# A table load at the head of every norm, in a kernel of three transformer layers

## The reference

```python
def rmsnorm(x, g):
    x32 = x.astype(jnp.float32)
    y = x32 * lax.rsqrt(jnp.mean(x32 * x32, axis=-1, keepdims=True) + EPS)
    return (y * g.astype(jnp.float32)).astype(x.dtype)
```

## Time and profile before

| | us |
|---|---|
| median of 3 runs | 2118.26 |
| lowest and highest run | 2116.7, 2118.72 |
| profiled execution, its own time | 2116.96 |
| its span, first to last instruction | 2115.2 |

### The profile page before, as it was taken

How to read it: one execution, slowest core, us unless ns; L and a number is a source line. 1 busy time by engine, 2 the same in 40 slices (tenths; PEclk the granted TensorE clock), 3 DMA queues, 4 the chain that set the end, 5 groups by cost and what they waited for, 6 DMA issues and landing times.

```text
span 2115.2 us, 39901 instructions
## 1 busy us (share of the span) xinstructions
PE 1879.0 (89%) x15218; PEld 1779.9 (84%) x15218; DVE 949.9 (45%) x1627; ACT 885.3 (42%) x1305; POOL 872.9 (41%) x446
## 2 busy tenths in 40 slices
PE   6985689999999998999999978996699975969997
PEld 6962589899999987899999978964699975759997
DVE  2025323783000087655555544245544438734444
ACT  4462325555555455444444443133244442014443
POOL 4300037988788899300000025200565654004553
PEclk9887899999999999999999999998899998989999
DMA  4471045454455577655555542200355533024553
GB/s 159 151 259 50 1 142 177 160 178 166 162 179 182 185 245 261 229 183 179 184 182 180 185 158 80 71 11 20 108 182 178 179 127 102 1 94 148 183 183 110
DMA packets 85339, 312.63 MB, mean 148 GB/s; under 512 B 9601, under 2 KB 9601, under 8 KB 84865
## 3 DMA queue, kind: packets, MB, share of 16 engines
q1 hardware_dynamic: 84960, 309.40, 43.4%
q0 software_dynamic: 288, 1.97, 0.2%
HBM read 310.28 MB, written 1.05 MB: 147 GB/s over the span
## 4 chain that ended last, share of the span: by engine, by line
PE 79%; POOL 6%; DVE 6%; issue 4%; ACT 3%; DMA 1%; SPq 0%; POOLq 0%; DVEq 0%; ACTq 0%
PE psr L656 40%; PE acc L656 23%; PE psr L645 4%; POOL sq L1918 4%; POOL wl L472 2%; PE psr L1016 2%; PE psr L885 1%; PE psr L634 1%; PE acc L712 1%; DMA ring<-in_ada_w 1%; DVE rinv L1448 1%; ACT wh L463 1%; PE psr L950 1%; DVE sq L1467 1%; DVE sq L1472 1%
## 5 line engine op out<-in xcount | busy, mean ns | idle before, releaser
L472 POOL TENSOR_TENSOR wl<-ring,wh 128x1024 fp32r<-128x1024 f32 x286 | 709.7, 2485 | 707.5 <-ACT wh L463 707.3
L463 ACT ACTIVATE wh<-ring 128x1024 fp32r<-128x1024 f32 x458 | 482.2, 1054 | 559.0 <-PE psr L656 497.7
L656 PE MATMUL psr<-hh,wh 128*128 128x256 f32 x2200 | 551.5, 288 | 66.0 <-DVE hl L1481 63.2
L656 PE MATMUL psr<-hl,wh 128*128 128x256 f32 x2200 | 550.0, 287 | 0.0
L656 PEld LDWEIGHTS psr<-hh,wh 128*128 128x128 f32 x2200 | 431.2, 196 | 69.1 <-issue 65.4
L656 PEld LDWEIGHTS psr<-hl,wh 128*128 128x128 f32 x2200 | 431.8, 196 | 0.0
L656 PE MATMUL psr<-hh,wl 128*128 128x256 f32 x2200 | 313.5, 286 | 9.7 <-POOL wl L472 9.7
L656 PEld LDWEIGHTS psr<-hh,wl 128*128 128x128 f32 x2200 | 287.4, 195 | 12.2 <-POOL wl L472 12.1
L472 DVE TENSOR_TENSOR wl<-ring,wh 128x1024 fp32r<-128x1024 f32 x172 | 213.5, 1241 | 183.3 <-ACT wh L463 183.1
L656 PE MATMUL acc<-hl,wh 128*128 128x256 f32 x1024 | 251.4, 284 | 0.0
L656 PE MATMUL acc<-hh,wl 128*128 128x256 f32 x1024 | 251.3, 284 | 0.0
(11 more groups left out here) (271 smaller groups left out, 2528.7 us busy)
## 6 DMA issues: line engine op xcount, KB each, us to landing
ring<-in_peer_u SPq DMA_DIRECT2D x128, 512.0 KB, 3.2
ring<-in_peer_v SPq DMA_DIRECT2D x128, 512.0 KB, 3.2
ring<-in_ada_w SPq DMA_DIRECT2D x96, 512.0 KB, 4.8
ring<-in_ffn_a SPq DMA_DIRECT2D x44, 512.0 KB, 3.9
ring<-in_ffn_b SPq DMA_DIRECT2D x44, 512.0 KB, 3.3
ring<-in_ffn_d SPq DMA_DIRECT2D x44, 512.0 KB, 3.2
ring<-in_pw SPq DMA_DIRECT2D x24, 512.0 KB, 3.2
ring<-in_w_in SPq DMA_DIRECT2D x18, 512.0 KB, 3.6
```

What stands on the lines that cost most here:

```text
L463: nc.scalar.activation(wh[:, q % 2, :], ring[:, s, :], ACT.Copy).then_inc(high_ready, 1)
L472: eng.tensor_tensor(wl[:, q % 2, :], ring[:, n % NS, :], wh[:, q % 2, :], ALU.subtract)\
L656: return mm(out, w, a, start=start, stop=stop, skip_group_check=True)
```

## The change

One line is added as the first statement of ACT's `norm`: an explicit load of the set that holds the square root. It comes ahead of the waits that are handed to the norm, and behind the waits that are written ahead of the call. `norm` is called 13 times.

```diff
             def norm(k, src, n, waits, prev=None, piece_ready=None):
 
+                nc.scalar.preload_act_table_set("sqrt_and_others")
                 for s, v in waits:
                     if v is None:
                         drained(act, s)
```

## The result

The changed kernel takes 2128.16 us (median of five runs, 2125.64 to 2132.76), the kernel before 2118.26 (five runs, 2111.42 to 2120.12). The ratio is 1.0049, with a 95% interval of 1.0034 to 1.0064: slower by 7.2 to 13.6 us, 10.4 in the middle. The forecast was +5.7. The profiled execution took 2125.64 us around a span of 2123.8, 8.6 more than before; it is the fastest of the five.

The account below looks back on a forecast made before the run. Bound: mostly line 656's matrix products on TensorE, with 13 norms as short serial links. Heads 5.30 plus repeats 2.70 less 2.32 for roots gave +5.7 on 2118.26, so 2123.9 us; range 2120.0 to 2126.8.

Parts of the forecast that it names:

- the 2.32 taken off for the roots: Norms 6, 9 and 11: no load before the root, so it begins 0.61, 1.16 and 0.55 us earlier.
- TensorE's clock: Rival: PE keeps the lower clock longer as products start later behind norms; 3 us above the forecast, 2127; chance 0.05.
- A load costs 1.30 at the head: Exposed loads at the heads of norms 0, 1, 4 and 10: 1.28 + 1.42 + 1.30 + 1.30 = 5.30 us.
- Repeats cost as much as switches: Norms 2, 3 and 7, set already there: each load taken at 1.30 us, adding 0.20 + 1.40 + 1.10 = 2.70.
- 1.10 at its place: Norm 7: a repeated load amid the products of line 656 delays PE's products by about 1.1 us.
- Six loads are hidden: Norms 5, 6, 8, 9, 11 and 12: the load runs while ACT waits for x, at cost 0.
- Norm 2: Repeated load delays the squares 1.4 us; sums end just after DVE is free, so the mean is only 0.20 later.
- All of it on the chain: Norms 6, 9 and 11: the whole 2.32 us gained reaches the products, since they wait for the reciprocal.
- late next is the mean: Norms 6, 9 and 11: with the load gone, the mean limits next, so no more than 2.32 us can be had.
- heads and repeats: Added cost of exposed loads, 5.30 us in norms 0, 1, 4, 10 and 2.70 in norms 2, 3, 7.

Follow-up runs that it names:

- hidden: Load added only in norms 5, 6, 8, 9, 11 and 12 of the kernel before: 2118.95 us, ratio 0.9997.
- hold8: Kernel before, with POOL's clearing of a tile and first six diagonal blocks moved behind norm 8's scaling: 2115.79 us, ratio 0.999.
- repeats: Load added only in norms 2, 3 and 7 of the kernel before, where the set is there already: 2118.67 us, ratio 1.0012.
- hold: Kernel of "hidden", with POOL's first subtraction behind norms 6, 9 and 11 waiting until DVE's scaling is done: 2118.71 us, ratio 1.0002.
- control: Kernel before, no edit, under another name for a second trace: 2117.72 us, ratio 1.0004.
- copy: Kernel before, with an unused ACT copy of 1280 elements at the head of norms 4 and 10, no load added: 2127.0 us, ratio 1.0045.
- fill: Kernel before with loads in norms 0, 1, 4 and 10, plus unused matmuls of constants ahead of the sums of norms 4, 10 and 11: 2121.81 us, ratio 1.002.
- after8: Kernel before, with POOL's clearing and first six diagonal blocks moved behind its first feed-forward part: 2112.93 us, ratio 0.9981.

## Why the prediction was right or wrong

The direction was right, and the size was not: +10.4 (7.2 to 13.6) against +5.7, and 2128.16 us against a range up to 2126.8. Two terms of the sum failed: the 2.32 taken off for the roots, and TensorE's clock, which had no term at all.

- **A load costs 1.30 at the head (right).** Norm 0: load at 8.10 and squares at 9.40, forecast 8.2 and 9.5. Norms 1 and 3: 1.41 each for 1.42 and 1.40. Norms 4 and 10: 1.29 each for 1.30. No load was issued ahead of its wait, and behind a load the squares begin 0.01 to 0.02 later.
- **Repeats cost as much as switches (right).** All 13 take 1283 ns. Norm 7 came to 1.12 for 1.10 at its place, though the traces show nothing of it left by norm 8: that the delay stays was assumed. Of the two sentences of the Trainium skill ("ScalarE: Activation LUTs", "What ACT_TABLE_LOAD costs") the trace agrees with the one that the whole slot is copied; its price "for every switch to a different set" is paid here without a switch too.
- **Six loads are hidden (right).** The run "hidden" has 0.9997.
- **Norm 2 (size wrong).** +0.20 was forecast and +1.16 came. The step was that the sums would end 1.10 behind their start, 0.17 behind DVE. They took 2.04, at PE's lower level, and so the mean was late by nearly all of the load. This is chance as far as the traces go: norm 2's sums are at 2.04 or 2.05 as well in "hidden" and "hold8", which put no load there, and at 1.10 in "repeats", which does and where the mean comes 0.21 later against norm 1's, as forecast.
- **"All of it on the chain", the roots (wrong).** The roots came 0.60, 1.16 and 0.55 earlier, as said. The step that failed is "late next is the mean": late next was DVE's first scaling operation, which cannot pass POOL's subtraction (L472). I had looked for what waits for the root and not for what stands beside the operation behind it. "hidden" shows the gain lost, "hold" shows it returning when POOL is moved. Only norm 11 kept it, in the changed kernel, since its mean was so late that POOL was nearly done. The term was -2.32 and should have been about 0 (-0.64 in the changed kernel).
- **TensorE's clock (no term in the sum).** I gave this 0.05 and 3 us, for products that start later behind a norm, and ended the range at 2126.8, just short of its 2127. It happened in the norms' own sums instead: +0.91, +1.69 and +1.53 in norms 4, 10 and 11, 4.13 in the trace (norm 1's 0.52 is chance, as said under "control"). "copy" shows that the delay does it in norms 4 and 10, and "fill" that matmuls in the gap undo it. The row was at hand: I read the sums' duration in the earlier trace rows, but not the granted clock of each norm's sums, nor how long PE idled ahead of them.

Made again, the sum is 8.00 for heads and repeats (6.9 where norm 7's is not kept), 0 for the roots, and up to 4.13 for the clock: 7 to 12, which holds the measured 10.4. As only one execution of each kernel was traced, this division is an estimate. That the total lies in the range does not prove each part.

What stays open: why norm 11's sums fall to the lower level when its own load is hidden and PE's idle time ahead of them is 2.5 us, as it is in the traces that have them at 3.69; why norm 10's do so in "hold" and "after8"; and how the clock's part divides among the norms over many executions.

## What to carry to other kernels

Put a table load where the engine is idle and ahead of its wait: below a wait it costs its full 1.3 us, above it nothing, and a load of the set that is there costs as much as any other. Before a gain on one link of a serial chain is counted, look at what the next engine does at its new, earlier time, and beside which other engine. Where PE pauses for some microseconds, read the granted clock of the matmuls behind the pause, in more than one execution, before a small delay is priced: a small delay may make them take half as long again, and a few matmuls of constants in the gap can be worth more than the edit.

## What the runs showed of the hardware that was not expected

- 0.5 us more of idle time ahead of norm 10's sums (4.11 against 3.60) took them from 3.69 to 5.38, and so did 1.2 and 1.3 us more (4.76 and 4.88); "hold" and "after8" did it with none at that place. So a forecast from one gap alone is not enough. In norm 1, behind the same work and the same gap of 1.08 us, the six sums take 1.53 in five traces and 2.90 in five.
- TensorE's lower level in and behind the norms costs this kernel some 14 us, and matmuls of constants in the gaps bring these back (2118.3 to 2104.3).
- Beside POOL's tensor-tensor operations, four of DVE with two inputs took 6.97 us (norm 8), and 2.50 alone (norm 10); in norm 9 the four ended 2.36 behind POOL's, whether they began 0.31 or 1.47 ahead of its end.
- Of two loads of the same set in a row one shows in the trace.
